# Token rows fetched first, modulation by pairs, and the first query tile multiplied between the modulation tiles

## The reference

```
shift, scale, gate = split(silu(c) @ w_mod + b_mod, 3)     # and the same of c_ctx for the context rows
hx = rmsnorm(x, g_pre) * (1 + scale) + shift
hc = rmsnorm(ctx, g_pre) * (1 + scale_c) + shift_c
q, k, v, ga, uf, ... = split(hx @ w_in)                    # and hc @ w_in
```

## Time and profile before

| | us |
|---|---|
| median of 3 runs | 2135.06 (2132.92 to 2140.09) |
| profiled execution, its own time | 2134.2 |
| its span | 2132.4 |
| PE busy | 2007.3 |
| first matmul of tile q 0 | 67.65 |
| end of tile q 1 on PE | 101.57 |

### The profile page before, as it was taken

How to read it: one execution, slowest core, us unless ns; L and a number is a source line. 1 busy time by engine, 2 the same in 40 slices (tenths; PEclk the granted TensorE clock), 3 DMA queues, 4 the chain that set the end, 5 groups by cost and what they waited for, 6 DMA issues and landing times.

```text
span 2132.4 us, 27302 instructions
## 1 busy us (share of the span) xinstructions
PE 2007.3 (94%) x10623; PEld 1668.5 (78%) x10623; DVE 737.1 (35%) x1707; ACT 870.1 (41%) x1636; POOL 827.4 (39%) x637
## 2 busy tenths in 40 slices
PE   5899989996998999998999999999998999999997
PEld 3788868875876988877788888888877788888886
DVE  4312075336125535437551111005537751111004
ACT  5321267635225735557532222212647723222211
POOL 5423255415345314430135444443530044444442
PEclk8999999998999999989999999999999999999999
DMA  9241133421223112320123332322330033333320
GB/s 287 81 121 60 50 99 100 119 50 40 80 79 99 61 45 86 119 86 10 41 79 99 99 99 86 113 94 76 121 113 21 21 86 93 99 97 83 117 99 40
DMA packets 206294, 183.74 MB, mean 86 GB/s; under 512 B 31670, under 2 KB 182572, under 8 KB 206168
## 3 DMA queue, kind: packets, MB, share of 16 engines
q1 hardware_dynamic: 200276, 170.73, 26.4%
q10 hardware_dynamic: 5892, 11.27, 1.6%
HBM read 179.86 MB, written 5.40 MB: 87 GB/s over the span
## 4 chain that ended last, share of the span: by engine, by line
PE 82%; DVE 8%; ACT 5%; issue 3%; POOL 2%; DMA 1%; ACTq 0%; SPq 0%; DVEq 0%
PE ps L1144 22%; PE ps L1146 22%; PE ps L1145 22%; PE ps L1622 3%; PE ps L1637 3%; PE ps L1238 2%; PE ps L1648 2%; PE ps L1188 2%; POOL w_lo L698 2%; PE ps L1226 1%; ACT w_hi L720 1%; PE ps L1216 1%; DMA raw<-in_w_mod 1%; DVE sc L2114 1%; DVE k_lo L1927 1%
## 5 line engine op out<-in xcount | busy, mean ns | idle before, releaser
L698 POOL TENSOR_TENSOR w_lo<-raw,w_hi 128x512 fp32r<-128x512 f32 x598 | 788.0, 1349 | 1218.7 <-ACT w_hi L720 1218.6
L720 ACT ACTIVATE w_hi<-raw 128x1024 fp32r<-128x1024 f32 (+2 forms) x309 | 307.2, 1037 | 255.4 <-PE ps L1146 244.5
L1144 PE MATMUL ps<-g_hi,w_lo 128*128 128x512 f32 (+1 forms) x928 | 352.9, 380 | 1.5 <-POOL w_lo L698 1.5
L1146 PE MATMUL ps<-g_hi,w_hi 128*128 128x512 f32 (+1 forms) x928 | 352.0, 379 | 0.0
L1145 PE MATMUL ps<-g_lo,w_hi 128*128 128x512 f32 (+1 forms) x928 | 352.0, 379 | 0.0
L1144 PEld LDWEIGHTS ps<-g_hi,w_lo 128*128 128x128 f32 x928 | 174.4, 188 | 38.7 <-issue 1.3
L1146 PEld LDWEIGHTS ps<-g_hi,w_hi 128*128 128x128 f32 x928 | 174.4, 188 | 36.2
L1145 PEld LDWEIGHTS ps<-g_lo,w_hi 128*128 128x128 f32 x928 | 174.4, 188 | 36.0
L1144 PE MATMUL ps<-h_hi,w_lo 128*128 128x512 f32 (+1 forms) x496 | 181.1, 365 | 0.1
L1145 PE MATMUL ps<-h_lo,w_hi 128*128 128x512 f32 (+1 forms) x496 | 176.2, 355 | 0.0
L1146 PE MATMUL ps<-h_hi,w_hi 128*128 128x512 f32 (+1 forms) x496 | 176.1, 355 | 0.0
(11 more groups left out here) (264 smaller groups left out, 3482.6 us busy)
## 6 DMA issues: line engine op xcount, KB each, us to landing
raw<-in_w_in SPq DMA_DIRECT2D x30, 1024.0 KB, 5.1
raw<-in_w_mod SPq DMA_DIRECT2D x24, 1024.0 KB, 5.2
raw<-in_w_gate SPq DMA_DIRECT2D x44, 512.0 KB, 4.0
raw<-in_w_up SPq DMA_DIRECT2D x44, 512.0 KB, 5.2
raw<-in_w_down SPq DMA_DIRECT2D x22, 1024.0 KB, 4.8
raw<-in_w_out SPq DMA_DIRECT2D x8, 1024.0 KB, 5.0
strips<-bias_rows ACTq DMA_DIRECT2D x18, 256.0 KB, 3.9
raw<-in_w_in SPq DMA_DIRECT2D x16, 256.0 KB, 4.7
```

What stands on the lines that cost most here:

```text
L698: pool.tensor_tensor(w_lo[:, i % SPLIT, a:e], raw_of(what)[:, a:e], w_hi[:, i % SPLIT, a:e].bitcast(F32), ALU.subtract).then_inc(s_tile_lo ...
L720: act.activation(w_hi[:, i % SPLIT, a:b], raw_of(what)[:, a:b], ACT.Copy).then_inc(s_tile_hi.sem, s_tile_hi.nth((what, n)))
L1144: pe.matmul(o, lhs[1], rhs[0], start=first, stop=False)
L1146: return pe.matmul(o, lhs[0], rhs[0], start=False, stop=last)
```

## The change

The token rows and context rows are loaded by the first three DMAs of SP, and all sixteen small vectors go through ACT's queue. ACT and DVE sum the squares and DVE normalizes all rows before the first modulation tile is split. The eight modulation tiles are used in the order 0, 4, 1, 5, 2, 6, 3, 7, so that each pair gives shift and scale of two blocks k; in `stream` tile q 0 stands before the last two. They have own buffers for hi and lo (`first_hi`, `first_lo`, five pairs laid over memory that is used later). The condition is repeated over 128 columns (`cond_rep`), so the product fills 128 rows and `fold` has 128 rows. Six tiles are multiplied, then the rows of q 0 are multiplied block by block, with the transposes of the next pair and the last two modulation tiles between them. The constants and the Fourier weights are loaded after q 1, before kv. The product for `wf` moves, in both layers, from the front of the layer to between kv and uf.

```diff
-        for j in range(8):
-            stream.append(mod_tile(0, j))
+        FIRST = [(0, "mod", j) for j in (0, 4, 1, 5, 2, 6, 3, 7)]
...
+                first = [mod_tile(0, j) for _, _, j in FIRST]
+                mix = first[:6] + mix[:1] + first[6:] + mix[1:]
+            stream += mix + [mod_tile(*m) for m in mods_in_attention[l]] + outs
         for l in range(DEPTH):
...
 
         def width(what):
...
-            for dst, src in vectors[::2]:
-                sp.dma_start(dst, src).then_inc(s_vectors.sem, 16)
+            sp.dma_start(res[:, 0:2, :], I["x"][0, 0:2 * P, :].rearrange("(t p) d -> p t d", p=P)).then_inc(s_x_landed[0].sem, 16)
+            sp.dma_start(res[:, 2:4, :], I["x"][0, 2 * P:4 * P, :].rearrange("(t p) d -> p t d", p=P)).then_inc(s_x_landed[1].sem, 16)
+            sp.dma_start(res_c[:], I["ctx"][0].rearrange("(t p) d -> p t d", p=P)).then_inc(s_x_landed[2].sem, 16)
             for n, (what, loads, _) in enumerate(stream):
                 if n >= RAW:
                     sp.wait_ge(s_tile_lo.sem, s_tile_lo.at(stream[n - RAW][0]))
...
+                    if stream[n - RAW][0] in FIRST:
+                        sp.wait_ge(s_first_lo.sem, s_first_lo.at(stream[n - RAW][0]))
+                if what == (0, "kv"):
+                    sp.wait_ge(s_mm.sem, s_mm.at(("tile", FIRST[7])))
+                    for dst, src in consts:
+                        sp.dma_start(dst, src).then_inc(s_consts.sem, 16)
+                    for dst, src in ((dft_ccos[:], I["dft_ccos"]), (dft_csin[:], I["dft_csin"])):
+                        sp.dma_start(dst, src).then_inc(s_wf_landed.sem, 16)
+                    sp.wait_ge(s_wf_zero.sem, s_wf_zero.at(0))
+                    for l in range(DEPTH):
+                        for h in range(2):
+                            sp.dma_start(wf[HD * h:HD * h + HD, l, :, HD * h:HD * h + HD],
+                                         I["w_fourier"][l].rearrange("(c h) a b -> h a c b", h=2)[h]).then_inc(s_wf_landed.sem, 16)
...
-                if n == RAW - 1:
-                    sp.dma_start(res[:], I["x"][0].rearrange("(t p) d -> p t d", p=P)).then_inc(s_x_landed.sem, 16)
-                    sp.dma_start(res_c[:], I["ctx"][0].rearrange("(t p) d -> p t d", p=P)).then_inc(s_x_landed.sem, 16)
-                if n == 9:
-                    for dst, src in consts:
-                        sp.dma_start(dst, src).then_inc(s_consts.sem, 16)
...
+            def first_lo_part(i):
+
+                what, hi, lo = FIRST[i], first_hi[first_slot[i]], first_lo[first_slot[i]]
+                pool.wait_ge(s_tile_hi.sem, s_tile_hi.at((what, 0)))
+                for a in range(0, POOL_COLS, PIECE):
+                    e = min(POOL_COLS, a + PIECE)
+                    pool.tensor_tensor(lo[:, a:e], raw_of(what)[:, a:e], hi[:, a:e].bitcast(F32),
+                                       ALU.subtract).then_inc(s_tile_lo.sem, s_tile_lo.nth(what))
...
+            for i in range(6):
+                first_lo_part(i)
+            tile_lo_part(0, 0)
+            ctx_lo(0, 0)
+            ctx_lo(0, 1)
+            tile_lo_part(0, 1)
+            ctx_lo(0, 2)
+            ctx_lo(0, 3)
+            first_lo_part(6)
+            tile_lo_part(0, 2)
+            first_lo_part(7)
+            ctx_lo(0, 4)
+            ctx_lo(0, 5)
+            tile_lo_part(0, 3)
+            ctx_lo(0, 6)
+            ctx_lo(0, 7)
+            pool.wait_ge(s_mm.sem, s_mm.at(("tile", FIRST[7])))
             pool.memset(wf[:], 0.0).then_inc(s_wf_zero.sem, s_wf_zero.nth(0))
...
+            for dst, src in vectors:
...
+            def first_hi_part(i):
+
+                what = FIRST[i]
+                if 3 <= i < 6:
+                    act.wait_ge(s_mm.sem, s_mm.at(("tile", FIRST[i - 3])))
+                wait_landed(act, what)
+                for n in range(2):
+                    a = HALF * n
+                    act.activation(first_hi[first_slot[i]][:, a:a + HALF], raw_of(what)[:, a:a + HALF],
+                                   ACT.Copy).then_inc(s_tile_hi.sem, s_tile_hi.nth((what, n)))
+                s_tile_hi.name_latest(what)
+
+            def first_row(i):
+
+                act.wait_ge(s_mm.sem, s_mm.at(("tile", FIRST[i])))
+                if i >= 2:
+                    act.wait_ge(s_mod.sem, s_mod.at(FIRST[i - 2]))
+                act.activation(mod_row[:, i % 2, :], ps[:, ROW_BANK[i], 0:256], ACT.Copy).then_inc(s_mod_row.sem, s_mod_row.nth(FIRST[i]))
...
+            def first_rows(m):
+
+                act.wait_ge(s_nt.sem, s_nt.at((0, 2 * m + 1)))
+                for k in (2 * m, 2 * m + 1):
+                    act.wait_ge(s_mod_x.sem, s_mod_x.at((0, k)))
+                    if k >= 4:
+                        act.wait_ge(s_lo_c.sem, s_lo_c.at((0, k - 4)))
+                    act.activation(tmp_x[:, tx(0, k), :], ps[:, 3, CTX * (k % 2):CTX * (k % 2) + CTX], ACT.Identity, scale=mod_a[:, 1, k:k + 1],
+                                   bias=mod[:, 1, k:k + 1]).then_inc(s_mod_c.sem, s_mod_c.nth((0, k)))
+                    act.wait_ge(s_mm.sem, s_mm.at(("tile", FIRST[3 + (4 * TOK * (k + 1) - 1) // (4 * TILE)])))
+                    act.activation(h_hi[:, k, 0:SEQ], tmp_n[:, k % 3, :], ACT.Copy).then_inc(s_hi.sem, s_hi.nth((0, "n", k)))
+                    ctx_hi(0, k)
+
+            act.wait_ge(s_x_landed[0].sem, 16)
+            squares(0, 0)
+            squares(0, 1)
+            act.wait_ge(s_x_landed[1].sem, 16)
+            squares(0, 2)
+            act.wait_ge(s_x_landed[2].sem, 16)
+            squares(0, 4)
+            root((0, "pre"), 8, NT)
+            for i in range(6):
+                first_hi_part(i)
+                if i >= 2:
+                    first_row(i - 2)
+            first_rows(0)
             split_next()
+            first_row(4)
+            first_row(5)
+            first_rows(1)
+            first_hi_part(6)
+            first_hi_part(7)
+            first_row(6)
+            first_rows(2)
+            first_row(7)
+            first_rows(3)
...
+            def first_mod(i):
+
+                what, o = FIRST[i], ps[:, ROW_BANK[i], 0:256]
+                hi, lo = first_hi[first_slot[i]], first_lo[first_slot[i]]
+                pe.wait_ge(*emptied[ROW_BANK[i]])
+                emptied[ROW_BANK[i]] = s_mod_in.after(i)
+                pe.wait_ge(s_tile_lo.sem, s_tile_lo.at(what))
+                pe.wait_ge(s_first_lo.sem, s_first_lo.at(what))
+                for part in range(2):
+                    for k in range(KD):
+                        m = pe.matmul(o, cond_rep[:, k, :], (lo, hi)[part][:, 256 * k:256 * k + 256], start=part == 0 and k == 0, stop=part == 1 and k == KD - 1)
+                m.then_inc(s_mm.sem, s_mm.nth(what))
+                left(what)
+
+            def first_turn(i):
+
+                pe.wait_ge(s_mod_row.sem, s_mod_row.at(FIRST[i]))
+                for c in range(2):
+                    m = pe.matmul(ps[:, ROW_BANK[i], 256 + 2 * c:258 + 2 * c], mod_row[:, i % 2, P * c:P * c + P], fold[:], start=True, stop=True)
+                m.then_inc(s_mod.sem, s_mod.nth(FIRST[i]))
...
+            def first_rows(k):
+
+                what = (0, "q", 0)
+                w = both_parts(begin(what), lambda r: r.rearrange("p (k c) -> p k c", k=KD))
+                need(what, 256 * (k + 1))
+                for part, n, a in ((0, SEQ, 0), (1, CTX, SEQ)):
+                    if part == 0:
+                        pe.wait_ge(s_lo.sem, s_lo.at((0, "n", k)))
+                    else:
+                        pe.wait_ge(s_lo_c.sem, s_lo_c.at((0, k)))
+                    for c in range(2):
+                        b = 4 + 2 * part + c
+                        if k == 0:
+                            pe.wait_ge(*emptied[b])
+                            emptied[b] = s_proj.after((0, ("q", 0), c, part))
+                        m = mm3(ps[:, b, 0:n], both_parts(w, lambda r: r[:, k, P * c:P * c + P]),
+                                both_parts((h_hi, h_lo), lambda r: r[:, k, a:a + n]), k == 0, k == KD - 1)
+                        if k == KD - 1:
+                            m.then_inc(s_mm.sem, s_mm.nth((0, ("q", 0), c, part)))
+                if k == KD - 1:
+                    left(what)
...
+            turn_pair(0)
+            first_mod(0)
+            for i in range(1, 6):
+                first_mod(i)
+                first_turn(i - 1)
+            first_turn(5)
+            first_rows(0)
+            turn_pair(1)
+            first_rows(1)
+            first_mod(6)
+            first_rows(2)
+            first_turn(6)
+            turn_pair(2)
+            first_rows(3)
+            first_mod(7)
+            first_rows(4)
+            first_turn(7)
+            turn_pair(3)
+            for k in range(5, KD):
+                first_rows(k)
 
...
+                if l == 0:
+                    pe.wait_ge(s_wf_landed.sem, 16 * (2 * DEPTH + 2))
+                pe.wait_ge(*emptied[6])
```

(65 more changed lines are left out.)

185 lines of the change are left out of this document (92 added, 93 removed).

## The result

The changed kernel takes 2142.85 us (median of 14 runs, 2138.04 to 2150.46), the kernel before 2133.02 in the same comparison (14 runs, 2130.47 to 2140.55). The ratio is 1.0043, with an interval of 1.0029 to 1.0056: slower, by 6 to 12 us. The time lies within the predicted 2132.5 to 2145.5, but not in its likeliest case (2135 to 2141.4); it lies in that of the second rival. As a difference the forecast was too small: 3.9 us over the kernel before, where the ratio says 9.2 (1.0043 of 2133.02).

The account below looks back on a forecast made before the run. The prediction took PE as busy 94% of the span, with only the first 101.57 us open. Profiled 2134.2 us plus 1.1 for the start and 3.7 for the wf products gave 2139.0, range 2132.5 to 2145.5.

Parts of the forecast that it names:

- likeliest case: Whole kernel: a start about as long as before and two exposed wf products, 2135 to 2141.4 us, chance 0.60.
- the second rival: PE from 50 to 80 us: low clock holds through the mixed stretch, 3 to 6 us more, 2142 to 2146, chance 0.23.
- Vectors at 8.8: Start, ACT's queue: sixteen vectors land at 7.8 alone, plus 1 us for sharing with the rows, so 8.8.
- Normalizations at 8.6 us: Start, DVE: six normalizations, one at 0.8 and five at 1.57 beside POOL, 8.6 us, ending at 25.1.
- The fourth tile at 32.0: Start, SP's loads: fourth modulation tile waits for DVE's lo at 27.0, plus 5 us to landing at 32.0.
- q 0 at 50.3: PE: block 0 of q 0 starts at 50.3, after a stretch where each wait is on the path.
- From 50.3 to 85.1, 34.8 us: PE to the end of q 0: 26.5 us work, 5 gap before tile seven, 3.3 low clock.
- At nothing: Behind q 1: later loads of constants and wf weights, the wider condition and the cond_rep copy cost nothing.
- q 1: PE: first piece some 0.6 us late, q 1 ends at 102.7, 1.1 us later than before.
- wf at 3.7: Between kv and uf in both layers: exposed product and copy, 1.85 us each, 3.7 us together.
- The sum: Whole kernel: 2134.2 + 1.1 + 3.7 = 2139.0 us, 3.9 over the median of 2135.06.
- the chance of slower (0.24): Whole kernel: slower by over 0.3%, above 2141.5 us: the second rival with the upper edge of the first, chance 0.24.

Follow-up runs that it names:

- Experiments 2: Changed kernel with the small vectors issued first and split over SP's and ACT's queues, rows behind them; ratio to the kernel before 1.0020.
- experiment 10: Changed kernel with SP waiting for all sixteen vectors before it issues the rows; vectors used 1.0 us after the issues end at 6.51, no ratio given.
- experiments 4 and 6: Changed kernel with 26 and 36 idle matmuls in PE's two gaps, 1.0011 (4); with the second pair's transposes ahead of q 0's block 0, 1.0006 (6).
- the edit alone: Kernel before with only the product for wf moved behind kv in both layers; ratio to the kernel before 1.0010.
- The second executions: Both kernels profiled once more, unchanged: span 2144.4 us for the changed kernel and 2130.6 us for the kernel before.
- the filled kernel before: Kernel before with 30 transposes that nobody reads in PE's wait of 3.52 us; ratio to the kernel before 0.9989.

## Why the prediction came out as it did

**Vectors at 8.8: the term that failed.** They came at 12.25. "From above they wait as long as one MiB moves", 10.8, was no bound: they came 4.2 us later after their last issue than they do alone. I had let them share the DMA engines with one MiB; of their packets the last moved at 11.3, and by 11.0 all three MiB of rows had gone ahead. The Trainium skill (DMA: Bandwidth & Descriptors, Queues, rings and completion order) says that a semaphore's increment lands only after every earlier write of that DMA engine, whichever queue it came from. Experiments 2 and 10 don't contradict that rule: used 1.0 to 1.5 us after the last issue with the rows behind them, 5.3 with the rows ahead. They don't show it either. By the packets of experiment 10 the data themselves were late, which sharing the DMA engines with the bulk would explain without it. Nor was it a wait for all that had been asked for before: the first modulation tile was issued at 2.24, and the last of its increments moved at 13.9, behind the vectors.

**Normalizations at 8.6 us: too dear.** The six took 6.5. Beside POOL they took 1.76 and 0.94 in alternation, where the prediction had 1.57 for each. That row was beside pieces of 512 columns only. POOL's share of a modulation tile is 640 columns, a piece of 512 and one of 128, and in both kernels DVE finished one normalization for each piece. The shorter pieces are what made them cheaper. So the turns of whole instructions that the prediction weighed do show, but with a 512 piece a turn costs 1.57 to 1.76 us and not the 2.0 of its sum. This gave back 2.1 of the 3.45 lost, the squares another 0.5, and DVE's first lo began 0.8 late (25.89 for 25.1).

**The fourth tile at 32.0** was split at 33.98: the 0.8, another 0.8 because DVE's first lo took 2.69 beside POOL and not 1.88, and 0.3 from the issue at 28.67 to the landing. "DMA idle for 7 us or more" was right; it was nine.

**q 0 at 50.3** was 52.46, which is the 2.0 of the fourth tile passed on whole and 0.2 more: nothing hides anything there.

**From 50.3 to 85.1, 34.8 us.** It took 35.1, from 52.46 to 87.57. The gap of 5 us before the seventh tile was 5.12, and experiments 4 and 6 showed both halves of the term: 3.0 to 3.1 for the clock, and the chain of the second pair as the cause of the gap. (The working was rounded in its favour: 7.6 less 2.1 is 5.5 and not 5, and one and a half blocks at 2.1 are 3.2.) The kernel before paid 0.5 to 0.8 of the same kind, inside its measured start.

**At nothing** was right: kv is split at 95.49 and starts at once behind the `hot,table` matmuls, and no wait for the constants shows.

**q 1** followed with 0.23 us of wait for 0.6 and ended at 104.87 for 102.7. So the start was 3.3 us longer and not 1.1, and the 2.2 that the forecast lacked come from the terms ahead of q 0.

**wf at 3.7** was 1.87 + 1.81 = 3.68 in the profile, and 1.88 and 1.81 with the edit alone.

**The sum.** With the start as measured the working gives 2134.2 + 3.3 + 3.7 = 2141.2; the profiled execution took 2142.74, the median 9.8 more than that of before. The second executions make the start's difference 4.5 in their pair, so 3.9 as a mean. Together with the products that is 7.6 of the 9.8, inside the interval of 6 to 12. The remaining 2 us are not pinned to a place, and the interval does not ask for them. Behind layer 1's product, from uf's first matmul there to the end of the span, the code is the same in all kernels. It took 1571.9 and 1569.9 us before, 1576.3 in the filled kernel before, and 1574.6 and 1572.9 after. In the other nine profiled executions it took 1570.4 to 1577.2, whatever was changed ahead of it. The means are 1572.7 for the three executions with the old order and 1573.0 for the eight with both products behind kv, so the change has no part there that these executions can show.

**The second rival**, low clock through the mixed stretch for 3 to 6 us more, gave the right time for a wrong reason: the clock cost 3.0 to 3.1, no more than in the forecast, and was back at 2.4 GHz from 70 on through q 1. So it is luck that the time lies in this rival's; what filled it were the late vectors above all, and some 2 us that no run places. The Trainium skill (TensorE: Matmul & The Clock Gate, HAM oscillation) describes matmuls that start at the low clock again behind each long wait for data. Here the trace agrees behind the gaps of 3.60 and 5.12 us, but the clock rose again within the work behind each (matmuls of 512 columns took 0.39 again from 57.74 and from 69.64 on), and dense work with turns of 0.5 us between the blocks ran at 2.4 GHz. The step that I got wrong was the bound on the vectors, and with it the chance of slower (0.24).
